# Low parts of the raw weight tiles of a block-product feed-forward layer: made by GpSimd arithmetic in place of a negated copy and an accumulating DMA

## The chip, the cores and the metric

The kernel runs on one core of a Trainium2 chip. The metric is the device time of one execution in microseconds (us). The kernel before took 2472.41 us (median of three runs, 2471.84 to 2474.03). A core has TensorE (matrix products into PSUM), VectorE, ScalarE and GpSimd (elementwise work in SBUF, the first two also on PSUM) and SyncE, which issues DMA transfers. ScalarE and GpSimd issue DMA transfers as well. The engines run side by side and wait for one another on semaphores.

## The reference

Two layers, each: x = x + 1/2 SwiGLU1(norm(x)); a mixer of a convolution module and windowed attention behind one input projection; x = x + 1/2 SwiGLU2(norm(x)). The part that the change touches is the first weight matrix of the four SwiGLU stages:

```python
def swiglu(h, w_in, w_out):
    gu = h @ w_in                              # 1024 -> 2 * 2816
    gate, up = gu[..., :D_FF], gu[..., D_FF:]
    return (jax.nn.silu(gate) * up) @ w_out    # 2816 -> 1024
```

There are 528 tokens (16 meta tokens and 512), D_MODEL is 1024, and everything is float32.

## The kernel before

**Split operands.** TensorE multiplies in a shortened float32 format (fp32r). Full precision is kept by splitting each operand v into a high part hi (v rounded to fp32r) and a low part lo = v - hi, and by three products, hi*hi, hi*lo and lo*hi. Tiles of weights are therefore held twice, in `wha`/`whb` (high) and `wla`/`wlb` (low).

**Seven block products.** The product with `w_in` goes by pairs j of 128 gate columns and 128 up columns, 22 pairs a stage and 4 stages, so 88 pairs. The pair and the tokens form a 2 by 2 block scheme that needs seven products P1 to P7 instead of eight (`seventh`, L1028 on), of 12 matmuls each (4 blocks of rows by 3 products of parts). The weights that enter them are either raw quarter tiles (P1 and P2 use two of them, "A"; P4 uses one, "A22") or sums of quarters ("S12", "S43"). `raw` is the buffer of the loaded quarters, two pairs deep.

**How each low part is made.** For the sums, VectorE adds the quarters (`sum12`, `sum43`, four additions at L1379, L1381, L1391, L1392), ScalarE rounds (`sum_hi`, L675), and VectorE subtracts (`sum_lo`, L1399). For A (128x1024) and A22 (128x512), ScalarE copies the raw tile into the high tile with rounding (L657, L666), then writes the negative of the high tile into the low tile (L659, L668), and GpSimd issues a DMA that adds the raw tile, read again from HBM, onto it (L584, L589). TensorE waits for these with `a_lo` ahead of P1 and with `a22_lo` ahead of P4.

**Order of the work.** Each engine has its own hand-written program, in order. In the iteration of pair j TensorE does P1(j), P2(j), P7(j-1), P5(j), P6(j), P4(j-1), P3(j). ScalarE does silu(j-1), the high part of S12(j+1), `copy_e1(j)` (L688, from PSUM, for P6), `base_hi(j+2)` (A), `copy_e5` (L693), the high part of S43(j+1), `copy_e6` (L698), `base22_hi(j+1)` (A22), `inner_hi`. VectorE does `sum12(j+1)`, `gate(j,0)` (L1459, L1469), `up2(j-1)` (L1477), `sum43(j+1)`, two `sum_lo`, `inner(j-1)` (L1485, L1487), `gate(j,1)` (L1467, L1469), `inner_lo` (L1493). GpSimd does `base_lo(j+2)` and `base22_lo(j+1)`. SyncE loads `raw` for pair j+2 (`load_pair`, two DMAs: L522 of 768 KB, L525 of 256 KB) once the readers of pair j are done.

**Chunks.** The 22 pairs of a stage come in chunks of 7, 7 and 8; behind each chunk 8 output blocks (L1078) follow, in which TensorE has 39 us or more of products. The mixer (L1020) comes behind stages 0 and 2 and loads its weights by DMAs from GpSimd's queue (L594, L598), which the change leaves as they are.

Of the kernel before, what the change touches and what calls it, by code (L numbers as in the profile page):

```python
# [248 lines left out]
def build(nc, x, params, qk_gain, sinks, pairs, outs7, outs8, mixes, out):  # L249
# [7 lines left out]
    with ctx:  # L257
# [3 lines left out]
        def sem(name):  # L261
            return ctx.enter_context(nc.semaphore(name))
# [115 lines left out]
        def units(bufs, u, n):  # L378

            t, u = (bufs[0], u) if u < BASE_UNITS else (bufs[1], u - BASE_UNITS)  # L380
            return t[:, u:u + n, :, :].rearrange("p u k c -> p (u k) c")
# [55 lines left out]
        w_hi, w_neg = [sem(f"w_hi{s}") for s in range(4)], sem("w_neg")  # L437
        w_lo = [sem(f"w_lo{s}") for s in range(4)]
        raw_in, raw22_in = [sem(f"raw_in{s}") for s in range(2)], [sem(f"raw22_in{s}") for s in range(2)]
        a_hi, a_neg, a_lo = sem("a_hi"), sem("a_neg"), [sem(f"a_lo{s}") for s in range(2)]  # L440
        a22_hi, a22_neg, a22_lo = sem("a22_hi"), sem("a22_neg"), [sem(f"a22_lo{s}") for s in range(2)]
        s_sum, s_hi, s_lo = sem("s_sum"), sem("s_hi"), sem("s_lo")
        ob_in, ob_hi, ob_lo = [sem(f"ob_in{s}") for s in range(3)], sem("ob_hi"), sem("ob_lo")
        b_done, t_step, x7_hi, x7_lo = sem("b_done"), sem("t_step"), sem("x7_hi"), sem("x7_lo")
# [66 lines left out]
        def _(sp):  # L511
# [4 lines left out]
            def load_pair(j):  # L516

                j0, j1 = run_of(j)
                if j - 2 >= j0:
                    sp.wait_ge(a_hi, j - 1)  # L520
                    sp.wait_ge(s_sum, 4 * (j - 1))
                sp.dma_start(raw[:, j % 2, KP:4 * KP, :], pairs[j, :, KP:4 * KP, :]).then_inc(raw_in[j % 2], 16)  # L522
                if j - 2 >= j0:
                    sp.wait_ge(a22_hi, j - 1)
                sp.dma_start(raw[:, j % 2, 0:KP, :], pairs[j, :, 0:KP, :]).then_inc(raw22_in[j % 2], 16)  # L525

            def load_out(s, c, m):
# [43 lines left out]
        def _(pool):  # L571
# [6 lines left out]
                                    base=0, pattern=[[-1, P]], channel_multiplier=1).then_inc(const_done, 1)  # L578

            def base_lo(j):
                pool.wait_ge(a_neg, j + 1)
                pool.dma_start(units(lo_units, U_A[REGION[j]], 2), pairs[j, :, KP:3 * KP, :], accum_op=ALU.add)\  # L584
                    .then_inc(a_lo[j % 2], 16)

            def base22_lo(j):
                pool.wait_ge(a22_neg, j + 1)
                pool.dma_start(units(lo_units, U_A22[REGION[j]], 1), pairs[j, :, 0:KP, :], accum_op=ALU.add)\  # L589
                    .then_inc(a22_lo[j % 2], 16)  # L590

            def mix_hi(l, n):
                pool.wait_ge(blk_used, mix_freed(l, n))
                pool.dma_start(mix_units(hi_units, n), mixes[l * NBLK + n, :, :, :]).then_inc(w_hi[n % 4], 16)  # L594

            def mix_lo(l, n):
                pool.wait_ge(w_neg, l * NBLK + n + 1)
                pool.dma_start(mix_units(lo_units, n), mixes[l * NBLK + n, :, :, :], accum_op=ALU.add)\  # L598
                    .then_inc(w_lo[n % 4], 16)

            def stage(s):
                for c, (ta, tb) in enumerate(CHUNKS):
# [32 lines left out]
        def _(act):  # L635
# [15 lines left out]
            def base_hi(j):  # L651

                act.wait_ge(raw_in[j % 2], 16 * (j // 2 + 1))
                if freed(j, "A"):
                    act.wait_ge(blk_used, freed(j, "A"))
                hi = units(hi_units, U_A[REGION[j]], 2)
                func(hi, raw[:, j % 2, KP:3 * KP, :], ACT.Copy).then_inc(a_hi, 1)  # L657
                act.wait_ge(a_hi, j + 1)
                func(units(lo_units, U_A[REGION[j]], 2), hi.bitcast(F32), ACT.Copy, scale=-1.0).then_inc(a_neg, 1)  # L659

            def base22_hi(j):
                act.wait_ge(raw22_in[j % 2], 16 * (j // 2 + 1))
                if freed(j, "A22"):
                    act.wait_ge(blk_used, freed(j, "A22"))
                hi = units(hi_units, U_A22[REGION[j]], 1)
                func(hi, raw[:, j % 2, 0:KP, :], ACT.Copy).then_inc(a22_hi, 1)  # L666
                act.wait_ge(a22_hi, j + 1)
                func(units(lo_units, U_A22[REGION[j]], 1), hi.bitcast(F32), ACT.Copy, scale=-1.0)\  # L668
                    .then_inc(a22_neg, 1)

            def sum_hi(j, part):

# [330 lines left out]
        def _(pe):  # L1003
# [57 lines left out]
                seventh("P7", j, x_bank(j), begin=False)  # L1061

            def last_product(j):
                pe.wait_ge(a22_lo[j % 2], 16 * (j // 2 + 1))
                pe.wait_ge(c22_taken, j + 1)
                seventh("P4", j, x_bank(j), begin=False)

# [15 lines left out]
            def ffn(l, f):  # L1083
                s, which = 2 * l + f, 2 * f
                for c, (ta, tb) in enumerate(CHUNKS):
# [10 lines left out]
                    for j in range(j0, j1):  # L1096
# [3 lines left out]
                            bank_free(6)  # L1100
                        if j > 2:
                            pe.wait_ge(c21_taken, j - 2)
                        pe.wait_ge(a_lo[j % 2], 16 * (j // 2 + 1))
                        if opening:
                            x7 = lambda part: lambda kp: pe.wait_ge(x7_lo, (s * KP + kp) * 2 + part)
                            early = range(KP - 1)
# [726 lines left out]
```

## Time and profile before

| what | value |
| --- | --- |
| median of the runs | 2472.41 us |
| profiled execution, its own time | 2471.28 us |
| span of its trace | 2469.5 us |
| TensorE busy | 2386.1 us (97%) |
| VectorE busy | 1719.2 us (70%) |
| ScalarE busy | 1225.9 us (50%) |
| GpSimd busy | 348.4 us (14%), nearly all of it DMA issue |
| DMA | 358.73 MB, mean 145 GB/s |

The trace is of one execution, so sums on it are made against 2471.28 us. "Idle before" is the time that an engine stood still before an instruction, with what released it.

### The profile page before, as it was taken

The page shows a single profiled execution, that of the slowest core. Times are in us where ns is not written, and L with a number is a line of the kernel's source. Part 1 is how long each engine was busy: PE and PEld are TensorE (multiplying, and loading weights), DVE is VectorE, ACT ScalarE, POOL GpSimd, SP SyncE. Part 2 cuts the span into 40 slices and gives each one's busy share as a digit, 9 for nine tenths or more (in the row PEclk, how much of TensorE's full clock was granted, in tenths as well). Part 3 has the DMA queues.
Part 4 walks back from the last instruction along what each step waited for, and adds up shares of the span by engine and source line. Part 5 has one row for each costly group of instructions (what it writes and reads, how often), then busy time and mean ns, then how long its engine had stood idle before and what let it go on. Part 6 is the DMA issues. An engine that isn't in the chain of part 4 may idle for free.

```text
span 2469.5 us, 43489 instructions
## 1 busy us (share of the span) xinstructions
PE 2386.1 (97%) x17865; PEld 2248.3 (91%) x17865; DVE 1719.2 (70%) x2730; ACT 1225.9 (50%) x1994; POOL 348.4 (14%) x457
## 2 busy tenths in 40 slices
PE   3999999999999989999989999999999999899999
PEld 3999999999999989999989999999888777889897
DVE  6767665788886467676777676747887855767584
ACT  6646453443445366455656454534434454646371
POOL 1101011121112211001001011111121122101010
PEclk9999999999999999999999999999999999999999
DMA  5756555666666956566637565556766688657482
GB/s 143 172 127 162 135 123 138 138 142 137 136 141 154 213 124 163 134 151 145 153 90 165 128 160 138 125 143 135 149 140 143 132 204 197 132 149 165 114 180 90
DMA packets 107190, 358.73 MB, mean 145 GB/s; under 512 B 12144, under 2 KB 12144, under 8 KB 106992
## 3 DMA queue, kind: packets, MB, share of 16 engines
q0 software_dynamic: 64512, 211.84, 42.6%
q1 hardware_dynamic: 42112, 143.77, 19.7%
q8 instruction: 142, 2.33, 0.4%
q14 instruction: 56, 0.46, 0.1%
q10 hardware_dynamic: 368, 0.33, 0.0%
HBM read 352.72 MB, written 2.10 MB: 144 GB/s over the span
## 4 chain that ended last, share of the span: by engine, by line
PE 88%; DVE 4%; ACT 3%; DMA 3%; issue 2%; ACTq 0%; POOL 0%; DVEq 0%
PE po L1020 29%; PE po L1037 21%; PE po L1078 19%; PE ptr L1037 8%; PE pov L1037 5%; DMA wla<-in_mixes 1%; PE pov L1233 1%; PE pov L1231 1%; PE ptr L1212 1%; PE pstat L1196 1%; DMA wha<-in_mixes 1%; PE pov L1168 1%; DVE rms L1448 1%; ACT whb L657 0%; PE pstat L1198 0%
## 5 line engine op out<-in xcount | busy, mean ns | idle before, releaser
L1020 PE MATMUL po<-xh,wha 128*128 128x264 f32 (+1 forms) x1408 | 347.9, 314 | 4.7 <-DMA wla<-in_mixes 4.2
L1020 PE MATMUL po<-xl,wha 128*128 128x264 f32 (+1 forms) x1408 | 338.5, 307 | 0.0
L1020 PE MATMUL po<-xh,wla 128*128 128x264 f32 (+1 forms) x1408 | 337.5, 306 | 0.0
L1580 DVE SCALAR_TENSOR_TENSOR cv<-ub,lp,cv 128x528 f32<-128x528 f32 (+1 forms) x480 | 333.3, 754 | 1.7
L1020 PEld LDWEIGHTS po<-xh,wha 128*128 128x128 f32 x1408 | 229.4, 190 | 20.9 <-issue 4.2
L1037 PE MATMUL po<-x7h,wha 128*128 128x264 f32 (+1 forms) x844 | 241.1, 286 | 2.5 <-ACT tmp L693 1.6
L1037 PE MATMUL po<-x7l,wha 128*128 128x264 f32 (+1 forms) x844 | 240.5, 285 | 0.0
L1037 PE MATMUL po<-x7h,wla 128*128 128x264 f32 (+1 forms) x844 | 240.1, 285 | 0.0
L1020 PEld LDWEIGHTS po<-xh,wla 128*128 128x128 f32 x1408 | 228.5, 190 | 11.4
L1020 PEld LDWEIGHTS po<-xl,wha 128*128 128x128 f32 x1408 | 229.3, 190 | 10.4
L648 ACT ACTIVATE wla<-wha 128x1024 fp32r<-128x1024 f32 x136 | 143.0, 1053 | 163.5 <-DMA wha<-in_mixes 163.3
L1037 PE MATMUL po<-x7h,whb 128*128 128x264 f32 (+1 forms) x692 | 197.9, 286 | 9.9 <-ACT tmp L693 6.2
L1037 PE MATMUL po<-x7l,whb 128*128 128x264 f32 (+1 forms) x692 | 196.9, 284 | 0.0
L1037 PE MATMUL po<-x7h,wlb 128*128 128x264 f32 (+1 forms) x692 | 196.5, 284 | 0.0
L594 POOL DMA_DIRECT2D wha<-in_mixes x136 | 76.0, 561 | 694.0 <-PE po L1020 631.8
L1037 PEld LDWEIGHTS po<-x7h,wha 128*128 128x128 f32 x844 | 159.7, 189 | 3.5 <-issue 2.5
L1078 PE MATMUL po<-hh,wha 128*128 128x264 f32 (+1 forms) x688 | 161.6, 303 | 0.0
L1078 PE MATMUL po<-hh,wla 128*128 128x264 f32 (+1 forms) x688 | 161.1, 302 | 0.0
L1078 PE MATMUL po<-hl,wha 128*128 128x264 f32 (+1 forms) x688 | 161.0, 302 | 0.0
L1037 PEld LDWEIGHTS po<-x7l,wha 128*128 128x128 f32 x844 | 160.1, 190 | 0.0
L1037 PEld LDWEIGHTS po<-x7h,wla 128*128 128x128 f32 x844 | 159.6, 189 | 0.0
L598 POOL DMA_DIRECT2D wla<-in_mixes x136 | 122.8, 903 | 160.2 <-ACT wla L648 159.4
(232 smaller groups left out, 6341.4 us busy)
## 6 DMA issues: line engine op xcount, KB each, us to landing
wha<-in_mixes POOLq DMA_DIRECT2D x136, 512.0 KB, 4.2
wla<-in_mixes POOLq DMA_DIRECT2D x136, 512.0 KB, 6.3
raw<-in_pairs SPq DMA_DIRECT2D x88, 768.0 KB, 5.1
wlb<-in_pairs POOLq DMA_DIRECT2D x46, 512.0 KB, 8.5
raw<-in_pairs SPq DMA_DIRECT2D x88, 256.0 KB, 6.7
wla<-in_pairs POOLq DMA_DIRECT2D x88, 256.0 KB, 6.6
wla<-in_pairs POOLq DMA_DIRECT2D x42, 512.0 KB, 8.5
wfa<-in_outs SPq DMA_DIRECT2D x48, 448.0 KB, 3.3
```

The costliest lines, as they stand in the source:

```text
L594: pool.dma_start(mix_units(hi_units, n), mixes[l * NBLK + n, :, :, :]).then_inc(w_hi[n % 4], 16)
L598: pool.dma_start(mix_units(lo_units, n), mixes[l * NBLK + n, :, :, :], accum_op=ALU.add)\
L648: func(mix_units(lo_units, n), mix_units(hi_units, n).bitcast(F32), ACT.Copy, scale=-1.0)\
L1020: ins = mm(po[:, 2 * out_slot + h, 0:width], w[:, k, :], v[:, k, t:t + width], start=begin and k == 0 and p == 0, stop=last and k == kt - ...
L1037: ins = mm(bank, a[:, kp, :], b[:, kp, cols7], start=begin and kp == 0 and p == 0, stop=kp == KP - 1 and p == 2, skip_group_check=True)
L1078: ins = mm(po[:, 2 * ps(m) + h, 0:width], a[:, k, :], b[:, k, t:t + width], start=k == 0 and p == 0, stop=k == n - 1 and p == 2, skip_grou ...
L1168: mm(qss[:, pos, :], qsq[:, tok0(pos):tok0(pos) + CHUNK, :].rearrange("p n j -> p (n j)"), halves[:, :], start=True, stop=True)
L1196: mm(s_win(i, h), q[r, :], kn[r, c:c + WIN], start=True, stop=True)
L1212: tr(ptr[:, h * P:(h + 1) * P], pw[:, (b + 1) % 2, at:at + WIN], ident[:, :])
L1231: mm(dst[h * HD:(h + 1) * HD], vw[:, pos - 1, :], cut(pt[:, h, :]), start=True, stop=False, skip_group_check=True)
L1233: mm(dst, vm[:, :], cut(ptm[:, :]), start=pos == 0, stop=True, skip_group_check=True).then_inc(pv_done, 1)
L1580: stt(cv[:, j, a:], u, w, cv[:, j, a:], ALU.mult, ALU.add).then_inc(conv_step, 1)
```

## The change

ScalarE no longer writes the negated high part, and GpSimd no longer issues the accumulating DMA. GpSimd instead subtracts the high tile from the raw tile, both in SBUF, and writes the low tile. The semaphores `a_neg` and `a22_neg` go; `a_lo` and `a22_lo` now count GpSimd's instructions. SyncE's reload of `raw` waits for the low parts instead of the high ones, because GpSimd now reads `raw`. The definitions of `mix_hi` and `mix_lo` move in the text only.

```diff
@@ load_pair (SyncE)
                 if j - 2 >= j0:
-                    sp.wait_ge(a_hi, j - 1)
+                    sp.wait_ge(a_lo, j - 1)
                     sp.wait_ge(s_sum, 4 * (j - 1))
                 sp.dma_start(raw[:, j % 2, KP:4 * KP, :], pairs[j, :, KP:4 * KP, :]).then_inc(raw_in[j % 2], 16)
                 if j - 2 >= j0:
-                    sp.wait_ge(a22_hi, j - 1)
+                    sp.wait_ge(a22_lo, j - 1)
...
@@ base_lo, base22_lo (GpSimd)
             def base_lo(j):
-                pool.wait_ge(a_neg, j + 1)
-                pool.dma_start(units(lo_units, U_A[REGION[j]], 2), pairs[j, :, KP:3 * KP, :], accum_op=ALU.add)\
-                    .then_inc(a_lo[j % 2], 16)
+                pool.wait_ge(a_hi, j + 1)
+                nc.gpsimd.tensor_tensor(units(lo_units, U_A[REGION[j]], 2), raw[:, j % 2, KP:3 * KP, :],
+                                        units(hi_units, U_A[REGION[j]], 2).bitcast(F32), ALU.subtract)\
+                    .then_inc(a_lo, 1)
 
             def base22_lo(j):
-                pool.wait_ge(a22_neg, j + 1)
-                pool.dma_start(units(lo_units, U_A22[REGION[j]], 1), pairs[j, :, 0:KP, :], accum_op=ALU.add)\
-                    .then_inc(a22_lo[j % 2], 16)
+                pool.wait_ge(a22_hi, j + 1)
+                nc.gpsimd.tensor_tensor(units(lo_units, U_A22[REGION[j]], 1), raw[:, j % 2, 0:KP, :],
+                                        units(hi_units, U_A22[REGION[j]], 1).bitcast(F32), ALU.subtract)\
+                    .then_inc(a22_lo, 1)
...
@@ base_hi, base22_hi (ScalarE)
                 func(hi, raw[:, j % 2, KP:3 * KP, :], ACT.Copy).then_inc(a_hi, 1)
-                act.wait_ge(a_hi, j + 1)
-                func(units(lo_units, U_A[REGION[j]], 2), hi.bitcast(F32), ACT.Copy, scale=-1.0).then_inc(a_neg, 1)
...
                 func(hi, raw[:, j % 2, 0:KP, :], ACT.Copy).then_inc(a22_hi, 1)
-                act.wait_ge(a22_hi, j + 1)
-                func(units(lo_units, U_A22[REGION[j]], 1), hi.bitcast(F32), ACT.Copy, scale=-1.0)\
-                    .then_inc(a22_neg, 1)
...
@@ last_product and ffn (TensorE)
-                pe.wait_ge(a22_lo[j % 2], 16 * (j // 2 + 1))
+                pe.wait_ge(a22_lo, j + 1)
...
-                        pe.wait_ge(a_lo[j % 2], 16 * (j // 2 + 1))
+                        pe.wait_ge(a_lo, j + 1)
```


GpSimd's program keeps its order. Its queue ahead of the third to the fifth pair of the first stage, before; `wla`/`wlb` are low tiles, 128x1024 is A and 128x512 is A22:

```order
L584 DMA wla<-in_pairs 128x1024 [waits a_neg]
L589 DMA wla<-in_pairs 128x512 [waits a22_neg]
L584 DMA wlb<-in_pairs 128x1024 [waits a_neg]
L589 DMA wla<-in_pairs 128x512 [waits a22_neg]
L584 DMA wla<-in_pairs 128x1024 [waits a_neg]
```

The same place now:

```order
L582 TENSOR_TENSOR wla<-raw,wha 128x1024 [waits a_hi]
L588 TENSOR_TENSOR wla<-raw,wha 128x512 [waits a22_hi]
L582 TENSOR_TENSOR wlb<-raw,whb 128x1024 [waits a_hi]
L588 TENSOR_TENSOR wla<-raw,wha 128x512 [waits a22_hi]
L582 TENSOR_TENSOR wla<-raw,wha 128x1024 [waits a_hi]
```

Each DMA issue has become one arithmetic instruction at the same place, which waits for the high part (`a_hi`) instead of the negated one.

ScalarE's program in one iteration in the middle of the first chunk, before; L657 and L666 make the high parts of the raw tiles, L659 and L668 the negated ones:

```order
L703 ACTIVATE tmp<-tmp 128x528 [waits h_done,gate_done]
L675 ACTIVATE whb<-wfb 128x1024 [waits s_sum]
L688 ACTIVATE tmp<-ptr 128x264 [waits c12_taken,blk_used]
L657 ACTIVATE wha<-raw 128x1024 [waits blk_used,raw_in1]
L659 ACTIVATE wla<-wha 128x1024 [waits a_hi]
L693 ACTIVATE tmp<-po 128x264 [waits c22_taken,blk_used]
L675 ACTIVATE whb<-wfb 128x1024 [waits s_sum]
L698 ACTIVATE tmp<-ptr 128x264 [waits c11_taken,blk_used]
L666 ACTIVATE wha<-raw 128x512 [waits blk_used,raw22_in0]
L668 ACTIVATE wla<-wha 128x512 [waits a22_hi]
L709 ACTIVATE hh<-tmp 128x528 [waits h_done]
L703 ACTIVATE tmp<-tmp 128x528 [waits h_done,gate_done]
```

ScalarE's program in the same iteration now; L660 and L667 make the high parts:

```order
L701 ACTIVATE tmp<-tmp 128x528 [waits h_done,gate_done]
L673 ACTIVATE whb<-wfb 128x1024 [waits s_sum]
L686 ACTIVATE tmp<-ptr 128x264 [waits c12_taken,blk_used]
L660 ACTIVATE wha<-raw 128x1024 [waits blk_used,raw_in1]
L691 ACTIVATE tmp<-po 128x264 [waits c22_taken,blk_used]
L673 ACTIVATE whb<-wfb 128x1024 [waits s_sum]
L696 ACTIVATE tmp<-ptr 128x264 [waits c11_taken,blk_used]
L667 ACTIVATE wha<-raw 128x512 [waits blk_used,raw22_in0]
L707 ACTIVATE hh<-tmp 128x528 [waits h_done]
L701 ACTIVATE tmp<-tmp 128x528 [waits h_done,gate_done]
```

The two negated copies are gone, and the rest stands in the same order.

## Rows read from the trace of the kernel before

**Rows 1.** The page: busy us, share of the span, instructions.
```profile
PE 2386.1 (97%) x17865; PEld 2248.3 (91%) x17865; DVE 1719.2 (70%) x2730; ACT 1225.9 (50%) x1994; POOL 348.4 (14%) x457
```

**Rows 2.** What TensorE waited for: us in total, times, longest.
```profile
PE ptr L1037 <- DVE tmp L1467: 24.2, 10, 6.2
PE ptr L1037 <- DMA wlb<-in_pairs: 15.6, 1, 15.6
PE ptr L1037 <- DVE x7l L1364: 13.0, 6, 7.8
```

**Rows 3.** One steady pair: us; busy PE, PEld, DVE, ACT, POOL; clock; DMA share; GB/s.
```profile
303.82:314.08 10.26, 10.26 (x86) 10.26 (x85) 8.22 (x14) 7.41 (x12) 1.73 (x2) 1.00 0.82 186
```

**Rows 4.** VectorE in that pair: start us, us, instruction [idle before].
```profile
303.82 0.43 DVE L1467 TENSOR_TENSOR tmp<-po,tmp 128x264 f32<-128x264 f32 x1 [0.46 <-PE po L1037]
304.29 0.43 DVE L1469 TENSOR_TENSOR tmp<-tmp,rms 128x264 f32<-128x264 f32 x1
...
305.97 0.69 DVE L1381 TENSOR_TENSOR wfb<-raw,wfb 128x512 f32<-128x512 f32 x1
308.12 0.43 DVE L1459 TENSOR_TENSOR tmp<-pov,tmp 128x264 f32<-128x264 f32 x1 [1.46 <-ACT tmp L688]
308.59 0.43 DVE L1469 TENSOR_TENSOR tmp<-tmp,rms 128x264 f32<-128x264 f32 x1
308.94 0.43 DVE L1477 TENSOR_TENSOR tmp<-po,tmp 128x264 f32<-128x264 f32 x1
309.28 0.68 DVE L1391 TENSOR_TENSOR wfb<-raw,wfb 128x512 f32<-128x512 f32 x1
...
310.49 2.44 DVE L1399 TENSOR_TENSOR wlb<-wfb,whb 128x1024 fp32r<-128x1024 f32 x2
312.84 0.43 DVE L1485 TENSOR_TENSOR tmp<-po,tmp 128x264 f32<-128x264 f32 x1
313.19 0.42 DVE L1487 TENSOR_TENSOR tmp<-tmp 128x264 f32<-128x264 f32 x1
```

**Rows 5.** ScalarE in that pair, the instructions around the two copies.
```profile
306.70 1.06 ACT L675 ACTIVATE whb<-wfb 128x1024 fp32r<-128x1024 f32 x1 [1.30 <-DVE wfb L1381]
307.66 0.37 ACT L688 ACTIVATE tmp<-po 128x264 f32<-128x264 f32 x1
307.93 1.05 ACT L657 ACTIVATE wha<-raw 128x1024 fp32r<-128x1024 f32 x1
309.01 1.06 ACT L659 ACTIVATE wla<-wha 128x1024 fp32r<-128x1024 f32 x1
...
312.67 0.63 ACT L666 ACTIVATE wha<-raw 128x512 fp32r<-128x512 f32 x1 [0.73 <-PE po L1037]
313.34 0.63 ACT L668 ACTIVATE wla<-wha 128x512 fp32r<-128x512 f32 x1
```

**Rows 6.** TensorE: the first matmul of P6 in that pair.
```profile
309.48 0.30 PE L1037 MATMUL po<-x7h,wha 128*128 128x264 f32 x1
```

**Rows 7.** GpSimd in that pair: its two DMA issues.
```profile
310.37 0.86 POOL L584 DMA_DIRECT2D wla<-in_pairs  x1 [5.50 <-ACT wla L659]
314.26 0.86 POOL L589 DMA_DIRECT2D wla<-in_pairs  x1 [3.03 <-ACT wla L668]
```

**Rows 8.** GpSimd's own operations: busy us, mean ns, idle.
```profile
L577 POOL TENSOR_SCALAR_AFFINE_SELECT ident<-ident 128x128 f32<-128x128 f32 x1 | 0.3, 283 | 0.2 <-POOL eps L575 0.2
L573 POOL MEMSET ident<- 128x128 f32 x1 | 0.2, 204 | 0.0
L572 POOL MEMSET eps<- 128x1 f32 x1 | 0.1, 98 | 0.3 <-POOLq L1824 0.3
```

**Rows 9.** TensorE behind its 6.2 us wait: us, busy, granted clock, DMA.
```profile
54.00:60.00 6.00, 4.92 (x22) 0.50 0.72 202
```

**Rows 10.** The page's DMA issues: queue, count, KB each, us to landing.
```profile
raw<-in_pairs SPq DMA_DIRECT2D x88, 768.0 KB, 5.1
wlb<-in_pairs POOLq DMA_DIRECT2D x46, 512.0 KB, 8.5
```

More of the change, by code:

```diff
@@ L439, in build @@
         raw_in, raw22_in = [sem(f"raw_in{s}") for s in range(2)], [sem(f"raw22_in{s}") for s in range(2)]
-        a_hi, a_neg, a_lo = sem("a_hi"), sem("a_neg"), [sem(f"a_lo{s}") for s in range(2)]
-        a22_hi, a22_neg, a22_lo = sem("a22_hi"), sem("a22_neg"), [sem(f"a22_lo{s}") for s in range(2)]
+        a_hi, a_lo, a22_hi, a22_lo = sem("a_hi"), sem("a_lo"), sem("a22_hi"), sem("a22_lo")
         s_sum, s_hi, s_lo = sem("s_sum"), sem("s_hi"), sem("s_lo")
@@ L582, in base_lo @@
             def base_lo(j):
-                pool.wait_ge(a_neg, j + 1)
-                pool.dma_start(units(lo_units, U_A[REGION[j]], 2), pairs[j, :, KP:3 * KP, :], accum_op=ALU.add)\
-                    .then_inc(a_lo[j % 2], 16)
+                pool.wait_ge(a_hi, j + 1)
+                nc.gpsimd.tensor_tensor(units(lo_units, U_A[REGION[j]], 2), raw[:, j % 2, KP:3 * KP, :],
+                                        units(hi_units, U_A[REGION[j]], 2).bitcast(F32), ALU.subtract)\
+                    .then_inc(a_lo, 1)
             def base22_lo(j):
-                pool.wait_ge(a22_neg, j + 1)
-                pool.dma_start(units(lo_units, U_A22[REGION[j]], 1), pairs[j, :, 0:KP, :], accum_op=ALU.add)\
-                    .then_inc(a22_lo[j % 2], 16)
[L592 to L599, printed above, removed]
+                pool.wait_ge(a22_hi, j + 1)
+                nc.gpsimd.tensor_tensor(units(lo_units, U_A22[REGION[j]], 1), raw[:, j % 2, 0:KP, :],
+                                        units(hi_units, U_A22[REGION[j]], 1).bitcast(F32), ALU.subtract)\
+                    .then_inc(a22_lo, 1)
             def stage(s):
@@ L617, in _, with mix_hi, mix_lo @@
             base_lo(1)
+            def mix_hi(l, n):
+                pool.wait_ge(blk_used, mix_freed(l, n))
+                pool.dma_start(mix_units(hi_units, n), mixes[l * NBLK + n, :, :, :]).then_inc(w_hi[n % 4], 16)
+            def mix_lo(l, n):
+                pool.wait_ge(w_neg, l * NBLK + n + 1)
+                pool.dma_start(mix_units(lo_units, n), mixes[l * NBLK + n, :, :, :], accum_op=ALU.add)\
+                    .then_inc(w_lo[n % 4], 16)
             for l in range(DEPTH):
```

## The prediction

> **What bounds the kernel now.** I read the busy table first: TensorE is busy 2386.1 us of the 2469.5 us span [rows 1], so what leaves TensorE's work as it is can take time away only from its waits. The list of those waits comes next: the largest are 24.2 us behind VectorE's L1467 (ten times, none over 6.2 us) and one of 15.6 us, the first of the kernel, behind the accumulating DMA for pair 0 [rows 2]. The second is the only one that the change addresses directly. Then I took one pair out of the middle of a chunk: its 10.26 us are TensorE's without a gap, at the full granted clock, and VectorE is busy for 8.22 us of them, ScalarE for 7.41 and GpSimd for 1.73 [rows 3]. Last, the timelines of that pair show how much room VectorE has. It stands still twice: 0.46 us ahead of L1467, until TensorE has finished P3, and 1.46 us ahead of L1459 [rows 4]. The reader is to see that only the first is room. The second is a chain that starts and ends on VectorE: L1381 makes the sum, ScalarE rounds it (L675, 1.06 us), copies E1 (L688, 0.37 us), and L1459 needs that copy [rows 4, 5]; it moves with VectorE. So the loop VectorE, ScalarE, VectorE takes 10.26 - 0.46 = 9.80 us of every 10.26 us. It is the second bound, 0.46 us behind the first. The same E1 copy also releases P6 on TensorE: it ends at 308.03 and P6 begins at 309.48, so VectorE may fall 1.45 us behind before TensorE stands [rows 5, 6].
>
> **What is removed.** From ScalarE 88 copies of 1.06 us and 88 of 0.63 us [rows 5], 149 us in all. In the pair none of it lies on the loop above: L659 follows E1's copy, L668 is behind P4 and followed by work with room. I count it as nothing there. From GpSimd 176 DMA issues of 0.86 us [rows 7] and their transfers. The steady pair waits for none of these [rows 3], so nothing again; the low part now comes sooner, and the rows show no one who waits for it but in the first pair. There the 15.6 us wait ends sooner, but TensorE also waits for x7l from VectorE, up to 7.8 us at once [rows 2], so the gain is what ScalarE's 1.06 + 0.63 + 1.06 us of removed copies give to that chain, between 0 and 2.75 us. I take 2.
>
> **What is added: the instructions.** GpSimd gets 88 subtractions of 128x1024 (A) and 88 of 128x512 (A22). The trace has no such operation. The nearest rows are GpSimd's affine select of 128x128 with one SBUF operand, 283 ns, and its memset of 128x1 and 128x128, 98 and 204 ns [rows 8]. From them: fixed part 0.1 us; (283 - 98)/127 = 1.46 ns a column for one operand read and one written; (204 - 98)/127 = 0.83 ns a column for a write alone. Upper bound, each operand read at the whole 1.46 ns: 2.92 ns a column, 3.09 and 1.59 us. Lower bound, VectorE's own subtraction: 1.22 us for A (L1399, 2.44 us for two) and 0.69 us for A22 (L1381's size) [rows 4]. One-operand rate: 1.6 and 0.84 us. I take the affine select's row and add one more pass over a port at the memset's price, 1.46 + 0.83 = 2.29 ns a column: 2.44 us for A and 1.27 us for A22. The Trainium skill, "GPSIMD Engine Reference", section "Elementwise — side-by-side cycle accounting", gives 4497 ns for a float32 tensor_tensor of 2048 columns; an estimate by it is 2.25 and 1.12 us, and the sum below would be about 16 us less.
>
> GpSimd has room: 3.7 us in 10.26. The low part of A(j+2) is due two iterations later and that of A22(j+1) one iteration later, so a late GpSimd is not the danger.
>
> **What is added: the place.** The question is whether GpSimd's reads hold up VectorE. Of VectorE's 14 instructions in the pair, ten take both operands from SBUF (L1469 twice, L1493, the four additions, L1399 twice, L1487); only L1459, L1467, L1477 and L1485 have one in PSUM. No row of before has GpSimd reading SBUF while VectorE works, so the cost is bounded from both sides: nothing, if the two do not touch, or the whole of GpSimd's instruction less what VectorE does meanwhile without a second SBUF operand. Against nothing speaks that VectorE reads two float32 SBUF operands a column at 1.19 ns (L1399) [rows 4], so it has no spare cycles on that side if a reader shares it. I take the upper end, as the likelier, for this reason. The Trainium skill, "SBUF — State Buffer", section "Who interferes with whom", states the mechanism: a VectorE instruction with two SBUF inputs contends with a GpSimd instruction that reads SBUF, and whoever starts first has the shared port for its whole length. No row here shows it yet; by the opposite rule, no contact, the sum would be the third case below.
>
> Step by step in the pair. L657 ends at 308.98 [rows 5]; GpSimd starts 0.3 us behind its releaser (L659 ends at 310.07, the issue starts at 310.37 [rows 5, 7]), so A's subtraction wants to start at 309.28. That is the very time at which VectorE's run of two-SBUF instructions begins, L1391 to the end of L1399 at 312.9 [rows 4]. If GpSimd is first, the run starts 2.44 us later; if VectorE is, GpSimd starts when L1485 (PSUM, 0.43) comes, and L1487 waits for the rest. Either way about 2.2 of the 2.44 us fall on VectorE. A22's subtraction follows L666, ready at about 313.6 in before's times; it covers one PSUM instruction of 0.43 us and costs 1.27 - 0.43 = 0.85 us. Together 3.05 us a pair, less the 0.46 us of room: 2.6 us. Behind VectorE's late L1381 stand ScalarE's L675 and L688, and P6 waits for them.
>
> How often: A's subtraction lies in the iterations with j+2 in the chunk, (5+5+6) x 4 stages = 64; in 12 more there is only A22's, 0.85 - 0.46 = 0.4 us each. The 12 chunks each first use up the 1.45 us buffer. Behind a chunk TensorE has 39 us and more of output products, where VectorE catches up. Sum: 64 x 2.6 = 166, + 5, - 17, - 2 at the start = +152 us. Against the profiled execution's own 2471.3 us, which is 1.1 us below the median of the runs: 2623 us, rounded 2620.
>
> **The reload of `raw`.** SyncE's two loads now wait for GpSimd. L522 waits in any case for the four additions of the same pair, one iteration after A's subtraction, and lands 5.1 us after issue [rows 10]; A22's load is put back by about 1.5 us, against a reader an iteration later. Nothing. If that cover went, L1379 would wait and the loop would grow by the same 1.5 us a pair.
>
> **The clock.** TensorE would stand 2.6 us in each pair. After its 6.2 us wait the granted clock was 0.50 over the 6 us window, that is 1.2 GHz for most of its matmuls [rows 9]. If that came after each short stand, some 3 us of matmuls would take twice as long, 1.5 us; TensorE has 2.6 us idle in the longer pair, so most of it is hidden. I add nothing, and the upper end has room for it.
>
> **Rivals.**
> Shared, not blocked: the two take turns, or GpSimd's instruction often falls into VectorE's 1.46 us gap, and half of the 3.05 us is paid. 1.5 - 0.46 = 1.07 us, x 64 = 68, - 17 = +50: about 2520 us. The tightly packed run L1391 to L1399 speaks against the gap being hit.
> No contact: VectorE's durations stay, TensorE stays gapless, and only the start moves: 2469 us. For it speaks only that no row shows contact.
> Faster: as before, and the first wait is the real head of the start. TensorE then begins after GpSimd's 2.44 us where an 8.5 us transfer stood [rows 10], 6 us earlier, of which I allow 3.5 us because VectorE's x7l is due in the same stretch, with ScalarE's 2.75 us on top: 6.3 us, 2465 us. It decides if VectorE is untouched and the start's chain runs through ScalarE all along. The waits for x7l at L1364, 13.0 us in six [rows 2], speak against it: what the first wait gives up, they would take.
>
> **How the numbers follow.** Blocked: 0.63. Shared: 0.18. No contact: 0.13. Faster: 0.06. The blocked case's own range comes from the price: with the one-operand rate 1.4 + 0.4 - 0.46 = 1.35 us a pair, +67 us, 2538; with VectorE's rate 0.8 us, +32 us, 2503; with the upper bound 3.6 us, +219 us, 2690. The range for 8 in 10 is 2490 to 2690: it holds the blocked and the shared case and leaves the two untouched cases out. A difference of 0.2% (5 us) is what a measurement of this kernel can tell from none. Faster by more: 0.05; within it: 0.13; slower: 0.82.
>
> **What would show it.** In a steady pair: a period near 12.9 us in place of 10.26; TensorE idle ahead of P6, put down to ScalarE's copy of E1; VectorE's L1391 or L1487 late or long behind GpSimd's subtraction, its PSUM instructions unchanged; GpSimd's subtractions near 2.4 and 1.3 us or longer. The output blocks and the mixer keep their time. A VectorE whose two-SBUF instructions keep 0.69 and 1.22 us back to back while GpSimd runs would prove the forecast wrong; a GpSimd instruction far from 2.44 us would move it along its range.

## The result and the profile after

The changed kernel takes 2590.11 us, median of 4 runs (2587.19 to 2591.21), against 2472.12 us (2467.57 to 2474.03) for the kernel before beside it: a ratio of 1.0469, 95% interval 1.0455 to 1.0482. It is slower by about 118 us. The forecast was 2620 us with a range of 2490 to 2690. In one experiment below, the placed and reordered kernel, one of five executions took 7676.4 us for a reason that nothing on record shows; its ratio is of the other four, and its median of all five is hardly moved by it.

The page of the changed kernel, busy times and the start of the chain that ended last, by engine:

```profile
PE 2413.4 (93%) x17865; PEld 2255.2 (87%) x17865; DVE 1901.8 (73%) x2730; ACT 1081.7 (42%) x1818; POOL 551.4 (21%) x457
...
PE 68%; DVE 17%; issue 10%; ACT 4%; DMA 1%; ACTq 0%; DVEq 0%; POOL 0%
```

Against [rows 1], VectorE has 183 us more of busy time with the same 2730 instructions. None of its instructions were changed, so they take longer. ScalarE is busy for 144 us less, about its removed copies, and GpSimd for 203 us more. TensorE's share of the chain is 68%, where it was 88%.

What TensorE waited for (us in total, times, longest), to be read against [rows 2]:

```profile
PE ptr L1035 <- DVE tmp L1465: 48.1, 30, 6.1
PE po L1035 <- DVE tmp L1465: 46.3, 38, 1.5
PE ptr L1035 <- DVE x7l L1362: 30.5, 6, 12.2
PE po L1035 <- ACT tmp L686: 23.5, 44, 0.6
PE ptr L1035 <- ACT tmp L686: 12.5, 20, 1.3
```

The wait of 15.6 us for the DMA is gone. The waits for x7l (the low part of the tokens' operand, made by VectorE) have grown from 13.0 to 30.5 us, which is about the two old ones together (28.6). Behind VectorE's L1465 (L1467 before) there are 68 waits with 94.4 us, where there were 10 with 24.2, and behind ScalarE's copy of E1 (L686) 64 with 36.0 us.

One steady pair, the same columns as [rows 3]:

```profile
320.04:332.52 12.48, 10.74 (x85) 10.34 (x85) 10.92 (x15) 5.82 (x10) 3.92 (x2) 1.00 0.28 86
```

The pair takes 12.48 us, where it took 10.26. TensorE is busy for 10.74 us of it, VectorE for 10.92 (8.22 before). TensorE stands in two places, ahead of P6 and then, five products later, ahead of P7:

```profile
320.00 0.39 PE L1035 MATMUL po<-x7h,whb 128*128 128x264 f32 x1 [0.53 <-ACT tmp L686]
328.79 0.36 PE L1035 MATMUL po<-x7h,whb 128*128 128x264 f32 x1 [1.23 <-DVE tmp L1465]
```

These are 1.76 us of the 2.22; most of the rest shows as busy time of TensorE (10.74 us, where it was 10.26). VectorE's timeline in that pair (start us, us, instruction, idle before), against [rows 4]:

```profile
320.04 0.43 DVE L1457 TENSOR_TENSOR tmp<-pov,tmp 128x264 f32<-128x264 f32 x1 [1.46 <-ACT tmp L686]
...
320.86 0.42 DVE L1475 TENSOR_TENSOR tmp<-ptr,tmp 128x264 f32<-128x264 f32 x1
321.20 2.72 DVE L1389 TENSOR_TENSOR wfa<-raw,wfa 128x512 f32<-128x512 f32 x1
...
324.44 2.43 DVE L1397 TENSOR_TENSOR wla<-wfa,wha 128x1024 fp32r<-128x1024 f32 x2
326.79 0.42 DVE L1483 TENSOR_TENSOR tmp<-ptr,tmp 128x264 f32<-128x264 f32 x1
327.13 1.17 DVE L1485 TENSOR_TENSOR tmp<-tmp 128x264 f32<-128x264 f32 x1
328.23 0.42 DVE L1465 TENSOR_TENSOR tmp<-po,tmp 128x264 f32<-128x264 f32 x1
...
332.52 0.43 DVE L1457 TENSOR_TENSOR tmp<-pov,tmp 128x264 f32<-128x264 f32 x1 [1.46 <-ACT tmp L686]
```

Only two instructions differ from before: the sum that starts at 321.20 (L1389, 0.68 us in [rows 4] as L1391) takes 2.72 us, and the second inner product's multiply (L1485, 0.42 us before as L1487) takes 1.17 us. The idle 1.46 us for ScalarE's copy is still there, and the idle 0.46 us ahead of L1465 is gone. GpSimd's timeline shows what stands beside the two:

```profile
320.97 2.39 POOL L582 TENSOR_TENSOR wlb<-raw,whb 128x1024 fp32r<-128x1024 f32 x1 [5.44 <-ACT whb L660]
326.49 1.52 POOL L588 TENSOR_TENSOR wla<-raw,wha 128x512 fp32r<-128x512 f32 x1 [3.12 <-ACT wha L667]
```

A's subtraction runs from 320.97 to 323.36. L1389 begins at 321.20 and ends 0.56 us behind it, at 323.92. A22's runs from 326.49 to 328.01, and L1485 ends 0.29 us behind it, at 328.30. The blocked time appears as a long VectorE instruction and not as idle time. Over the whole span, by line (busy us, mean ns, idle):

```profile
L1389 DVE TENSOR_TENSOR wfb<-raw,wfb 128x512 f32<-128x512 f32 x46 | 86.7, 1884 | 0.1
L1485 DVE TENSOR_TENSOR tmp<-tmp 128x264 f32<-128x264 f32 (+1 forms) x88 | 85.1, 967 | 0.0
```

L1389 has 106 us more than before for its 88, and L1485 48 us. In a chunk's first iteration A's subtraction comes a little later. In 8 of the 12 chunks it falls on L1390 instead, 18 us in all. In the other 4, the openings of the stages, it costs VectorE nothing: in the first it runs from 43.87 to 46.26, and VectorE stands from 43.36 to 46.12 in any case, behind ScalarE. So A's subtraction meets VectorE in 60 iterations and not in 64. These three lines are 172 of the 183 us.

The second and third chunks of a stage lose evenly in stages 1 to 3. The output blocks' first matmul behind the chunk (L1078, L1076 now), in the two traces:

```
                          before      now   lost since the chunk before
stage 1, chunk 1 (7)      121.09   128.58     7.5
stage 1, chunk 2 (7)      235.43   252.94    10.0
stage 1, chunk 3 (8)      360.32   390.04    12.2
...
stage 4, chunk 3 (8)     2422.50  2541.35
```

In brackets is the number of pairs. A chunk of 7 has 5 iterations with A's subtraction and one of 8 has 6: 5 x 2.22 = 11.1 and 6 x 2.22 = 13.3 us, each about 1.1 us above what the second and the third chunk lost. The first chunks lose less, 7.5, 5.4, 7.1 and 6.5 us, in part because their opening iteration loses nothing. In stage 4, whose pairs are narrower (256 columns a block), a pair took 9.88 us before and takes 12.44 now (2350.06 to 2362.50), and its second and third chunks lose 11.5 and 14.1 us. The output block itself keeps its 39.46 us. At the last chunk the two traces stand 118.85 us apart, the whole difference of the spans.

### The profile page after: what moved, and what is told of

It reads as the page before. It is cut to its first block, busy times and chain, and to the rows that moved or that the text cites. A ratio compares the mean times of both kernels' runs of the same rounds, so it can differ in the third digit from the quotient of the medians.

```text
span 2588.3 us, 43313 instructions
## 1 busy us (share of the span) xinstructions
PE 2413.4 (93%) x17865; PEld 2255.2 (87%) x17865; DVE 1901.8 (73%) x2730; ACT 1081.7 (42%) x1818; POOL 551.4 (21%) x457
## 4 chain that ended last, share of the span: by engine, by line
PE 68%; DVE 17%; issue 10%; ACT 4%; DMA 1%; ACTq 0%; DVEq 0%; POOL 0%
PE po L1018 29%; PE po L1076 18%; PE po L1035 9%; PE ptr L1035 5%; DVE tmp L1485 2%; DVE hl L1491 1%; DVE wfb L1389 1%; PE pov L1035 1%; ACT tmp L686 1%; PE pov L1231 1%; DVE tmp L1465 1%; DVE wfa L1389 1%; DVE wfb L1379 1%; PE pov L1229 1%; DVE tmp L1467 1%
## 5 line engine op out<-in xcount | busy, mean ns | idle before, releaser
L588 POOL TENSOR_TENSOR wla<-raw,wha 128x512 fp32r<-128x512 f32 x88 | 134.5, 1529 | 416.7 <-ACT wha L667 416.7
L582 POOL TENSOR_TENSOR wlb<-raw,whb 128x1024 fp32r<-128x1024 f32 x46 | 116.0, 2521 | 343.5 <-ACT whb L660 343.5
L582 POOL TENSOR_TENSOR wla<-raw,wha 128x1024 fp32r<-128x1024 f32 x42 | 103.9, 2475 | 370.2 <-ACT wha L660 370.2
L1035 PEld LDWEIGHTS po<-x7h,whb 128*128 128x128 f32 x692 | 131.0, 189 | 52.6 <-issue 26.5
L673 ACT ACTIVATE wha<-wfa 128x1024 fp32r<-128x1024 f32 x84 | 89.0, 1060 | 198.5 <-DVE wfa L1390 112.1
L1076 PE MATMUL po<-hh,wha 128*128 128x264 f32 (+1 forms) x688 | 161.6, 303 | 0.0
```

The lines of the kernel that those rows point to most:

```text
L582: nc.gpsimd.tensor_tensor(units(lo_units, U_A[REGION[j]], 2), raw[:, j % 2, KP:3 * KP, :], units(hi_units, U_A[REGION[j]], 2).bitcast(F32) ...
L588: nc.gpsimd.tensor_tensor(units(lo_units, U_A22[REGION[j]], 1), raw[:, j % 2, 0:KP, :], units(hi_units, U_A22[REGION[j]], 1).bitcast(F32), ...
L673: func(units(hi_units, u, 2), units(f32_units, u, 2), ACT.Copy).then_inc(s_hi, 1)
L1035: ins = mm(bank, a[:, kp, :], b[:, kp, cols7], start=begin and kp == 0 and p == 0, stop=kp == KP - 1 and p == 2, skip_group_check=True)
L1076: ins = mm(po[:, 2 * ps(m) + h, 0:width], a[:, k, :], b[:, k, t:t + width], start=k == 0 and p == 0, stop=k == n - 1 and p == 2, skip_grou ...
```

## Experiments

Ratios are to the kernel before, run beside each on the same chip, with 95% intervals. That kernel's medians there were 2475.5 to 2476.3 us.

**Does GpSimd's reading block, or its working at all?** Both subtractions become writes of a constant. The low parts of the raw tiles are left out (they are zero; TensorE's products with them stay), and so are the reads.

```
-    nc.gpsimd.tensor_tensor(lo, raw, hi, ALU.subtract)
+    nc.gpsimd.memset(lo, 0.0)
```

> The changed kernel with a GpSimd memset of the low tile in place of each subtraction, at the same place and behind the same wait; the low parts of the raw tiles are left out (zero). GpSimd then writes SBUF and reads nothing. Theory (VectorE's second SBUF operand waits for GpSimd's reads): L1389 and L1485 are back at 0.68 and 0.43 us, a steady pair takes 10.26 us, and the time is before's less what the removed copies and DMAs give back at the openings of the stages and the end of the mixer, some 10 us: 2462 us, 2455 to 2468. Rival (any work of GpSimd in SBUF, writes too, holds VectorE up): memsets of about 0.95 and 0.5 us each take most of their length from VectorE, 0.5 us or more a pair above the room, 2475 to 2500 us.

Measured: 2458.39 us, ratio 0.9939 (0.9924 to 0.9954). GpSimd's groups (busy us, mean ns, idle), then VectorE's timeline in a pair:

```profile
L586 POOL MEMSET wla<- 128x512 f32 x88 | 46.3, 526 | 460.9 <-ACT wha L663 460.9
L582 POOL MEMSET wlb<- 128x1024 f32 x46 | 44.6, 969 | 363.2 <-ACT whb L656 363.2
```

```profile
313.28 0.43 DVE L1453 TENSOR_TENSOR tmp<-pov,tmp 128x264 f32<-128x264 f32 x1 [1.46 <-ACT tmp L682]
...
314.44 0.68 DVE L1385 TENSOR_TENSOR wfa<-raw,wfa 128x512 f32<-128x512 f32 x1
...
318.33 0.42 DVE L1481 TENSOR_TENSOR tmp<-tmp 128x264 f32<-128x264 f32 x1
319.22 0.43 DVE L1461 TENSOR_TENSOR tmp<-po,tmp 128x264 f32<-128x264 f32 x1 [0.46 <-PE po L1031]
...
323.53 0.43 DVE L1453 TENSOR_TENSOR tmp<-pov,tmp 128x264 f32<-128x264 f32 x1 [1.46 <-ACT tmp L682]
```

GpSimd still works 0.97 and 0.53 us in each pair, from the same releasers. VectorE's two instructions (314.44 and 318.33) have their old 0.68 and 0.42 us, its idle 0.46 us is back, and the pair takes 10.25 us (313.28 to 323.53). A's memset lies beside L1385 here too (314.19 to 315.15), and over the span no L1385 takes more than 0.69 us. So what costs is the reading. The run also puts a number on everything that the change removes: about 15 us by the ratio.

**The two halves alone.** In each, one tile's low part is made by GpSimd and the other by the negated copy and the accumulating DMA of before.

```
e2: A   by GpSimd;  A22 by  func(lo22, hi22, ACT.Copy, scale=-1.0) + pool.dma_start(..., accum_op=ALU.add)
e3: A22 by GpSimd;  A   by  the same two
```

> The changed kernel with A22's low part made the old way (negated copy and accumulating DMA); only A (128x1024) by GpSimd. Theory: the loop over VectorE and ScalarE is 9.80 us plus the 2.03 us by which L1389 waits, so 11.8 us a pair; 64 x 1.57 = 100, less about 1.2 us of buffer in each of 12 chunks, less some 8 us given back elsewhere: 2549 us, 2535 to 2560. Rival (the two subtractions share their cost, or the slowing is a general one that grows with GpSimd's busy share): a cost in proportion to 2.4 of 3.9 us, 62% of 118 us, 2545 us for the time, but then L1389 is slowed by less than 2 us and other instructions by something.

> The changed kernel with A's low part made the old way; only A22 (128x512) by GpSimd. Theory: 0.75 us more on L1485 against 0.46 us of room, 0.29 us a pair over 76 pairs, nearly all of it inside the 1.45 us buffer of each chunk: 2470 to 2482 us, near 2475. Rival (cost in proportion to GpSimd's busy time, 1.5 of 3.9 us, 38% of 118 us): 2517 us.

Measured: A alone 2548.52 us, ratio 1.0301 (1.0286 to 1.0316); A22 alone 2478.06 us, 1.001 (1.0 to 1.0019). VectorE with A alone, then with A22 alone:

```profile
308.26 0.69 DVE L1380 TENSOR_TENSOR wfa<-raw 128x512 f32<-128x512 f32 x1
...
312.29 2.72 DVE L1392 TENSOR_TENSOR wfa<-raw,wfa 128x512 f32<-128x512 f32 x1
...
319.99 0.69 DVE L1380 TENSOR_TENSOR wfb<-raw 128x512 f32<-128x512 f32 x1
```

```profile
309.14 0.43 DVE L1459 TENSOR_TENSOR tmp<-pov,tmp 128x264 f32<-128x264 f32 x1 [1.46 <-ACT tmp L688]
...
310.30 0.68 DVE L1391 TENSOR_TENSOR wfb<-raw,wfb 128x512 f32<-128x512 f32 x1
...
314.20 1.18 DVE L1487 TENSOR_TENSOR tmp<-tmp 128x264 f32<-128x264 f32 x1
...
319.60 0.43 DVE L1459 TENSOR_TENSOR tmp<-pov,tmp 128x264 f32<-128x264 f32 x1 [1.46 <-ACT tmp L688]
```

Each subtraction lengthens its own VectorE instruction and leaves the other's alone. With A the pair takes 11.73 us (308.26 to 319.99). With A22 it takes 10.46 us (309.14 to 319.60), only 0.20 more than before, so some 0.55 of its 0.75 us is room. Alone they lose 73 and 2.5 us, together 118, which is 42 us more than the sum. The room, 0.55 us x 60 = 33 us, is there for each case alone but only once for the two. The same holds of the chunks' buffers; that the remaining 9 us are theirs is argued, and no run shows it.

**Is one operand enough to block?** GpSimd copies the raw tile into the low part, without subtracting the high part (left out), so it reads one SBUF operand.

```
-    nc.gpsimd.tensor_tensor(lo, raw, hi, ALU.subtract)
+    nc.gpsimd.tensor_copy(lo, raw)
```

> The changed kernel with a GpSimd copy of the raw tile into the low tile in place of each subtraction (the low part is then the whole raw tile, not the rest of it): one SBUF operand read, one written. Theory (the wait is GpSimd's whole instruction less about 0.4 us): whatever a copy takes, L1389 gets longer by its length less 0.4 us. At the affine select's rate of 1.46 ns a column, 1.6 and 0.84 us, L1389 takes 1.9 us, a pair 11.3 us, about 2520 us; at the memset's rate, 0.96 and 0.52 us, L1389 takes 1.3 us and the time is near 2470 us. Rival (only a GpSimd instruction with two SBUF operands is in VectorE's way): L1389 stays at 0.68 us, 2458 us.

Measured: 2465.06 us, ratio 0.9952 (0.9939 to 0.9964). VectorE, then GpSimd, in one pair:

```profile
318.16 1.35 DVE L1385 TENSOR_TENSOR wfa<-raw,wfa 128x512 f32<-128x512 f32 x1
...
322.73 0.50 DVE L1481 TENSOR_TENSOR tmp<-tmp 128x264 f32<-128x264 f32 x1
```

```profile
317.93 1.04 POOL L582 CAST wlb<-raw 128x1024 fp32r<-128x1024 f32 x1 [5.42 <-ACT whb L656]
322.07 0.87 POOL L586 CAST wla<-raw 128x512 fp32r<-128x512 f32 x1 [3.10 <-ACT wha L663]
```

Yes: the sum at 318.16 takes 1.35 us, and ends 0.54 us behind the copy. But the copy of A is 1.04 us, where 1.6 was expected; with one operand GpSimd needs 1.0 ns a column, with two 2.3. This copy is nearly as long as the memset (1.04 and 0.96 us) and stands at the same place, so it is not GpSimd's length that decides whether VectorE waits, but that it reads. What falls on VectorE, 0.67 + 0.08 us, is little more than the room: the pair takes 10.44 us, 0.18 more than before, and the removed parts pay for it.

**Can the reads be put where VectorE stands still?** A's subtraction waits for the last addition of `sum12` (L1382 in this run), so that it starts in the 1.46 us of idle time, and A22's waits for the inner product, so that it meets the old 0.46 us.

```
 for j in range(j0, j1):
     if j + 1 < j1:
+        if j > j0: pool.wait_ge(h_done, j)
         base22_lo(j + 1)
     if j + 2 < j1:
+        pool.wait_ge(s_sum, 4 * (j + 2) + 2)
         base_lo(j + 2)
```

> The changed kernel with the same GpSimd subtractions at other moments: A's waits for the sum L1379, so that it starts in VectorE's 1.46 us gap, and A22's, now ahead of A's in the queue, waits for L1485, so that it starts beside VectorE's PSUM instruction L1465. Theory (a lock held for GpSimd's whole instruction, paid only where VectorE wants its second SBUF operand): A's 2.4 us exposes about 0.5 us on L1467 and A22's about 0.3 us, 0.8 less the 0.46 us of room, about 0.35 us a pair, nearly all inside the chunks' buffers: 2460 to 2480 us, near 2467. Rival (GpSimd slows VectorE wherever it runs, by sharing bandwidth or by its length): the time stays near 2590 us.

Measured: 2501.63 us, ratio 1.0108 (1.0091 to 1.0125), a miss by 35 us. VectorE, then GpSimd:

```profile
322.44 0.69 DVE L1382 TENSOR_TENSOR wfa<-raw,wfa 128x512 f32<-128x512 f32 x1
324.59 0.43 DVE L1460 TENSOR_TENSOR tmp<-pov,tmp 128x264 f32<-128x264 f32 x1 [1.46 <-ACT tmp L689]
325.06 0.85 DVE L1470 TENSOR_TENSOR tmp<-tmp,rms 128x264 f32<-128x264 f32 x1
...
330.40 0.43 DVE L1468 TENSOR_TENSOR tmp<-po,tmp 128x264 f32<-128x264 f32 x1
330.86 1.29 DVE L1470 TENSOR_TENSOR tmp<-tmp,rms 128x264 f32<-128x264 f32 x1
```

```profile
323.21 2.41 POOL L582 TENSOR_TENSOR wla<-raw,wha 128x1024 fp32r<-128x1024 f32 x1 [2.32 <-DVE wfa L1382]
330.56 1.30 POOL L588 TENSOR_TENSOR wla<-raw,wha 128x512 fp32r<-128x512 f32 x1 [4.95 <-DVE tmp L1488]
```

A's part went as meant: it costs L1470 0.42 us and not 2.04. The mistake is in A22's. The idle 0.46 us ahead of L1468 was counted twice, as cover for A22's subtraction and again as room, but it exists only while TensorE is the bound. As soon as A's 0.42 us and the first part of A22's had used it up, VectorE ran without it, GpSimd's whole 1.30 us fell on L1470, 0.86 us, and the pair stayed at 10.96 us (322.44 to 333.40). Still, the same two subtractions cost some 90 us less than in the changed kernel, by their place alone.

The next attempt also changes VectorE's order, so that a multiply with an operand in PSUM stands where each subtraction ends.

```
-    gate(j, 0);  up2(j - 1)                        gate(j, 0):  PSUM product | between() | x rms
+    gate(j, 0, between=up2(j - 1))                 up2 / the second half of inner stand at between()
-    inner(j - 1);  gate(j, 1)
+    inner_first(j - 1);  gate(j, 1, between=inner_second(j - 1))
```

> The changed kernel with every subtraction still on GpSimd, placed where VectorE wants no second SBUF operand. A's starts in the 1.46 us gap behind L1379; A22's, ahead of it in the queue, behind the last L1397 (s_lo). VectorE's PSUM instructions are drawn together: up2 (L1475) ahead of the gate's multiply, and the gate's second PSUM sum (L1465) ahead of L1485. Theory (paid only where a second SBUF operand is wanted): A exposes some 0.1 us, A22 some 0.45 us, the loop is about 10.3 us against TensorE's 10.26, and what the write-only kernel gave back is kept: 2455 to 2472 us, near 2462, faster than before. Rival (a GpSimd subtraction costs VectorE more than this wherever it runs): 2490 us or more.

Measured: 2499.15 us, ratio 1.0086 (1.0072 to 1.0099), another miss: it is slower than before, not faster. Since it changes two things, VectorE's new order was also run alone, on the kernel before.

> The kernel before with VectorE's two reorderings of the placed kernel alone. Control: its loop keeps its length, so 2468 to 2477 us, no difference. Were the reorderings worth something by themselves, it would be faster, and the placed kernel's gain not GpSimd's.

Measured: 2484.08 us, ratio 1.0033 (1.0022 to 1.0045). TensorE's new wait, and VectorE's L1507 (mean ns, idle, releaser), on the kernel before with that order:

```profile
PE ptr L1037 <- DVE tmp L1481: 11.9, 12, 1.2
```

```profile
L1507 DVE SCALAR_TENSOR_TENSOR hl<-tmp,hh 128x528 fp32r<-128x528 f32 (+1 forms) x88 | 62.0, 705 | 36.5 <-ACT hh L709 36.5
```

The order costs 8 us by itself. VectorE now stands 0.37 us in each pair for ScalarE's high part of h. At a chunk's end the last up2 comes behind that (233.89 against 233.17 us at the second chunk's end), and TensorE waits 1 us for it, 12 times. In the placed and reordered kernel the pair takes 10.74 us (313.09 to 323.83), A's subtraction costs 0.20 us (L1473, 0.62 us for 0.42) and A22's 0.63 (L1501, 1.06 for 0.43). That is near the 0.1 and 0.45 us expected, and of the 0.48 us over 10.26 the order's own idle time can account for 0.37. Whether a better order would hide the two subtractions stays open.

**Is GpSimd at least better than VectorE itself?** The subtractions run on VectorE, and its other instructions keep their order.

```
-    nc.gpsimd.tensor_tensor(lo, raw, hi, ALU.subtract)
+    tt(lo, raw, hi, ALU.subtract)        # nc.vector, ahead of L1389 (A) and behind the second gate (A22)
```

> The changed kernel with the same subtractions on VectorE itself, A's behind L1475 (up2), A22's behind the second gate; GpSimd does none. Theory (a GpSimd subtraction costs VectorE nearly its whole length): VectorE pays 1.14 us for A and 0.61 us for A22 (instructions back to back) instead of 2.04 and 0.75 us of waiting, the loop is 9.80 + 1.75 = 11.55 us, 1.3 us a pair over before: 64 x 1.3 = 83, less 14 for the chunks' buffers, less 12 given back: 2530 us, 2515 to 2550, faster than the changed kernel. Rival (GpSimd does relieve VectorE, and the loss lies elsewhere, in the lateness of the low parts or the reload of raw): 2590 us or more.

Measured: 2545.49 us, ratio 1.0283 (1.0265 to 1.0302). VectorE in one pair:

```profile
322.85 0.43 DVE L1438 TENSOR_TENSOR tmp<-pov,tmp 128x264 f32<-128x264 f32 x1 [1.46 <-ACT tmp L651]
...
324.01 1.22 DVE L1336 TENSOR_TENSOR wla<-raw,wha 128x1024 fp32r<-128x1024 f32 x1
...
330.19 0.69 DVE L1341 TENSOR_TENSOR wla<-raw,wha 128x512 fp32r<-128x512 f32 x1
...
334.28 0.43 DVE L1438 TENSOR_TENSOR tmp<-pov,tmp 128x264 f32<-128x264 f32 x1 [1.46 <-ACT tmp L651]
```

They add 1.13 and 0.60 us of VectorE's time a pair (start to start), and the pair takes 11.43 us (322.85 to 334.28). On GpSimd they add 2.04 and 0.75 us to VectorE. With this placing, VectorE loses more by having them done beside it than by doing them.

**What are the removed copies worth?** The write-only run had given back some 15 us, where I had counted 2. The kernel before has a wait that [rows 2] does not show, for ScalarE's copy of E5, another PSUM tile of the block scheme (us, times, longest):

```profile
PE po L1037 <- ACT tmp L693: 7.8, 12, 0.7
```

ScalarE's order puts L659, the negated copy of A, ahead of that copy (L693). In this run it is moved behind it; all else is the kernel before.

```
 def base_hi(j):  ... func(hi, raw, ACT.Copy).then_inc(a_hi, 1)
-    act.wait_ge(a_hi, j + 1);  func(lo, hi, ACT.Copy, scale=-1.0).then_inc(a_neg, 1)
+def base_neg(j):  (the same two)     # called behind the copy of E5, and behind std() at a stage's opening
```

> The kernel before with one edit: ScalarE's negated copy of A (L659) stands behind the copy of E5 (L693) and behind the square root of a stage's opening, not ahead of them. Everything else, DMAs included, as before. Theory on what the removed copies gave back: TensorE's 12 waits for L693, 7.8 us in all, one in each chunk's first pair, go, and each of four openings is up to 1 us shorter: 2460 to 2466 us. Rival (the gain of the write-only kernel comes from the DMA traffic taken away, or from the start): 2470 us or more.

Measured: 2463.43 us, ratio 0.9947 (0.9933 to 0.996), 0.5% faster than the kernel before. TensorE's waits:

```profile
PE ptr L1050 <- DVE tmp L1480: 22.1, 10, 6.0
PE ptr L1050 <- DMA wlb<-in_pairs: 15.3, 1, 15.3
PE ptr L1050 <- DVE x7l L1377: 12.8, 5, 7.8
```

The 12 waits for the copy of E5 are gone, while the start's two (15.3 and 12.8 us) stand as before. The wait that goes is 7.8 us, about the 8.0 by which the spans of the two traces differ (2469.5 and 2461.5). The medians of the executions side by side differ by 12. The rest might lie at the openings of the stages, where the copy is now behind the square root too, but no run took that move alone. The DMAs are all still there, so the rival that laid the gain to the traffic is refuted for most of it. What the removed copies are worth is mostly their place in ScalarE's queue and not their 149 us. The negated copy of A22 was then moved in the same way, behind the high part of h.

> The kernel before with both negated copies moved back in ScalarE's program: A's (L659) behind the copy of E5 as in the last run, and A22's (L668) behind the high part of h (L709). Theory: the first move carries the gain (9 to 12 us); L668 stood ahead of L709 and L703, on which TensorE waits only at the chunks' ends, so the second adds 0 to 3 us: 2458 to 2465 us. Rival (L668's place matters as L659's did, another 0.6 us in each chunk and opening): 2455 us or less.

Measured: 2463.78 us, ratio 0.995 (0.9935 to 0.9966). The second move adds nothing that can be measured.

## Why the prediction was right, step by step

**The mechanism held.** It was: GpSimd's reads hold up VectorE's instructions with two SBUF operands, the loop VectorE, ScalarE, VectorE becomes the bound, and TensorE stands. The trace shows the long L1389 and L1485, unchanged PSUM instructions (0.42 and 0.43 us), and TensorE's waits for L686 and L1465. The write-only run shows that it is the reading: 0.68 us beside a write, 2.72 beside a read of two operands, 1.35 beside a read of one. The Trainium skill, "SBUF — State Buffer", section "Who interferes with whom", says that a GpSimd instruction which only writes does not contend with such a VectorE instruction and one that reads does, and that the shared ports are an exclusive lock. The runs agree with both. One sign was only half foreseen. The prediction has TensorE stand ahead of P6, for the copy of E1; there it stands 0.53 us in the pair shown, and 1.23 us ahead of P7, for L1465, since both blocks fall between L1457 and L1465.

**The sizes.** GpSimd's subtractions were put at 2.44 and 1.27 us; they are 2.39 and 1.30 us (where A22's runs without VectorE in its way). The Trainium skill, "GPSIMD Engine Reference", section "Elementwise — side-by-side cycle accounting", had led to an estimate of 2.25 and 1.12 us, so my figure from the rows was nearer. (By the prediction's own terms that estimate takes 0.34 us off each of 64 pairs, 22 us and not the 16 stated.) On VectorE I had counted 2.2 and 0.85 us and found 2.04 and 0.75. The predicted period was 12.9 us; 9.80 + 2.04 + 0.75 = 12.59, and 12.48 is measured. The loop was read 0.1 us too long: with A alone the pair is 11.73 and not 11.84 us, with both on VectorE 11.43 and not 11.53. Once VectorE no longer stands ahead of L1465, that instruction starts 0.07 us ahead of the end of the one before it (328.23 against 328.30), an overlap that the idle time had hidden. So the room was some 0.56 us and not 0.46. The pair loses 2.22 us and not 2.6, which over 64 iterations is worth 24 us.

**The copies on ScalarE were not worth nothing.** This step was wrong. I looked at one steady pair, where L659 follows E1's copy and hides. In the first pair of each chunk it does not: it stands ahead of the copy of E5 (12 waits, 7.8 us), and at the openings of the stages ahead of the square root. The removed parts give back about 15 us together (0.61%), and moving L659 alone gives 0.53% already; the two intervals overlap.

**The start.** I expected it 2 us earlier. The wait for the DMA went, but TensorE then waits for x7l, 30.5 us in all; its third such wait ends at 30.18 us, and ended at 29.09 before. In the write-only run it ends at 27.75 us. So what is removed does bring the start forward, by 1.3 us, near the 2 expected; but the subtractions for the first pairs also hold up the VectorE instructions that make x7l, and put it back by 2.4. In the changed kernel the first of these, 0.43 us before, stands beside A's subtraction for pair 0 (9.24 to 11.60):

```profile
9.82 2.07 DVE L1353 TENSOR_TENSOR tmp<-tmp 128x264 f32<-128x264 f32 x1 [1.56 <-ACT tmp L717]
```

The prediction looked for blocks in the pairs alone. The rival "faster", which had the first wait as the head of the start, is refuted by the write-only run: 1.3 us sooner and not 6, although VectorE is untouched there.

**The buffers and the sum.** Each chunk was to absorb 1.45 us before TensorE stands, 17 us in all. The table above shows 1.1 us a chunk, and 0.65 of that is the wait for E5's copy that no longer comes. So the buffers are worth some 0.45 us a chunk, 5 us in all, and that term was wrong too. The sum by measured terms has 60 iterations, 15 of them in stage 4: 45 x 2.22 + 15 x 2.56 = 138, + 3 for the 12 iterations with A22's alone (my estimate), + 2 for the blocks at the start, - 15 for the removed parts, - 5 for the buffers, = 123. Measured are 118; where the last 5 lie stays open. The forecast was too high by the price of a pair (24 us), the 4 openings (9) and what the removed parts give back (13), and too low by stage 4 (5) and the buffers (12). The mechanism was no luck, but that the total came within 30 us owes something to errors that cancel.

**Nothing, as predicted:** the additions that read `raw` did not wait for its reload (L1377 has no idle time), and it lands sooner than the 5.1 us in [rows 10]:

```profile
raw<-in_pairs SPq DMA_DIRECT2D x88, 768.0 KB, 4.2
```

The clock shows 1.00 in the pair above although TensorE stands 1.7 us in it. The output blocks kept their time.

**The rivals.** "Shared" (2520 us) would have needed subtractions that fall into the 1.46 us gap. In the steady pair A's starts 0.9 us behind the gap's end (320.97 against 320.04) and meets the run of sums. When the placed run put it into the gap, the time came to 2501.63 us, on this rival's side; but the cost there too is the whole overlap with an instruction of two SBUF operands, not a sharing. "No contact" is refuted by the 2.72 us of L1389.

## What to carry to other kernels

Before work is given to GpSimd, look at what VectorE does at that time. If GpSimd reads SBUF and starts first, VectorE loses GpSimd's length from the start of its own two-SBUF instruction on, less about 0.13 us, and here that was more than doing the work itself. If it must go there, make it wait for the instruction ahead of a known gap (which here brought 2590 down to 2502 us, still above the kernel before), and do not count a gap that another engine's bound has made. And look at the first pair of a loop as well as at a steady one: a harmless copy may stand there ahead of the one that is waited for.

## What the runs showed that I had not expected

The size of the block follows one rule in every run with reads: VectorE's instruction ends at GpSimd's end plus its own length less 0.13 us. Over all lengthened instructions of the changed kernel's trace the last term lies between 0.12 and 0.14 us. The changed kernel: 323.36 + 0.68 - 0.13 = 323.91 (323.92 measured). One operand: 318.97 + 0.68 - 0.13 = 319.52 (319.51). Placed: 331.86 + 0.43 - 0.13 = 332.16 (332.15).

It also works the other way. A22's subtraction takes 1.52 us in the changed kernel, where it starts at 326.49 while L1397 reads two SBUF operands until 326.87, and 1.30 us in the placed run, where it starts beside an instruction with an operand in PSUM (L1468). Its end follows the same rule: 326.87 + 1.30 - 0.16 = 328.01. So the one that comes later stands, whichever engine it is on.

The landings of the loads became shorter once the accumulating DMAs were gone, 5.1 to 4.2 us for 768 KB. Before, ScalarE's L657 had waited for `raw` 4 times, 4.7 us in all, and no longer does; no run shows whether anything was gained by it.
